# Narrow units of a two-block transformer kernel: eight high matmuls, then eight low ones

## What is computed

```python
p = einsum("bsd,de->bse", rms_norm(h), w_in)            # 2048 x 5120, then gates and two causal convolutions
h = h + rms_norm(einsum("bse,ed->bsd", mixed, w_out))   # 2048 x 2048
z = square(relu(einsum("bsd,df->bsf", m, w_up)))        # 2048 x 8192
h = h + rms_norm(einsum("bsf,fd->bsd", z, w_down))      # 8192 x 2048
# second block: w_in_a 2048 x 4096, pooling, 4 group matrices 512 x 512, w_out_a, w_k, w_v,
# w_in_b 2048 x 8192 (queries of 3 dilated attentions and a gate), attention, w_out_b
```

## Time and profile before

| | |
|---|---|
| median of 3 runs | 2077.09 us |
| profiled execution | 2077.38 us |
| its span, first to last instruction | 2075.6 us |
| TensorE matmul busy | 2035.1 us (98%), 11624 matmuls |
| weight loads busy, beside the matmuls | 1784.1 us (86%) |
| VectorE, ScalarE busy | 1410.5 us (68%), 1013.9 us (49%) |
| mean granted TensorE clock | 0.996 |

### The profile page before, as it was taken

How to read it: one execution, slowest core, us unless ns; L and a number is a source line. 1 busy time by engine, 2 the same in 40 slices (tenths; PEclk the granted TensorE clock), 3 DMA queues, 4 the chain that set the end, 5 groups by cost and what they waited for, 6 DMA issues and landing times.

```text
span 2075.6 us, 28620 instructions
## 1 busy us (share of the span) xinstructions
PE 2035.1 (98%) x11624; PEld 1784.1 (86%) x11624; DVE 1410.5 (68%) x1729; ACT 1013.9 (49%) x1348; POOL 9.8 (0%) x19
## 2 busy tenths in 40 slices
PE   6999999999999999999999999999999999999998
PEld 6999988988888888888879888788888888888886
DVE  5999956764655556555576766557577888887754
ACT  4676565544444444444454555445444455454542
POOL 0000000000000000000000000000000000000000
PEclk9999999999999999999999999999999999999999
DMA  6655646766666665666645565656566444544573
GB/s 219 195 185 164 193 136 226 234 200 192 194 190 195 189 194 188 190 194 189 195 132 183 162 194 186 226 172 223 188 191 192 153 160 145 183 146 160 179 261 107
DMA packets 305859, 384.27 MB, mean 185 GB/s; under 512 B 11673, under 2 KB 237209, under 8 KB 303936
## 3 DMA queue, kind: packets, MB, share of 16 engines
q1 hardware_dynamic: 305536, 382.22, 57.5%
q10 hardware_dynamic: 192, 0.23, 0.0%
HBM read 378.20 MB, written 4.19 MB: 184 GB/s over the span
## 4 chain that ended last, share of the span: by engine, by line
PE 93%; DVE 2%; issue 2%; ACT 1%; DMA 1%; SPq 0%; POOL 0%; DVEq 0%; POOLq 0%; ACTq 0%
PE job_banks L522 31%; PE job_banks L525 16%; PE job_banks L565 10%; PE job_banks L567 10%; PE job_banks L566 10%; PE job_banks L494 3%; PE job_banks L493 3%; PE job_banks L495 3%; PE aux_banks L747 1%; DMA raw_weights<-in_w_in 1%; ACT weights_high L812 1%; PE aux_banks L602 1%; DVE weights_low L1204 1%; PE aux_banks L567 0%; PE aux_banks L566 0%
## 5 line engine op out<-in xcount | busy, mean ns | idle before, releaser
L1204 DVE TENSOR_TENSOR weights_low<-raw_weights,weights_high 128x1024 fp32r<-128x1024 f32 x696 | 841.7, 1222 | 506.9 <-ACT weights_high L812 501.6
L812 ACT ACTIVATE weights_high<-raw_weights 128x1024 fp32r<-128x1024 f32 x696 | 728.3, 1056 | 621.7 <-PE job_banks L525 258.1
L522 PE MATMUL job_banks<-act_a,weights_high 128*128 128x512 f32 (+1 forms) x2048 | 610.1, 381 | 15.1 <-DVE weights_low L1204 6.6
L525 PEld LDWEIGHTS job_banks<-act_a,weights_low 128*128 128x128 f32 x2000 | 368.7, 191 | 74.1
L525 PE MATMUL job_banks<-act_a,weights_low 128*128 128x256 f32 (+1 forms) x2000 | 388.5, 276 | 0.0
L522 PE MATMUL job_banks<-act_b,weights_high 128*128 128x512 f32 x1088 | 345.6, 399 | 0.4 <-DVE value L1221 0.4
L522 PEld LDWEIGHTS job_banks<-act_a,weights_high 128*128 128x128 f32 x2048 | 315.2, 192 | 18.2 <-DVE weights_low L1204 9.7
L565 PE MATMUL job_banks<-weights_high,act_b 128*128 128x512 f32 x736 | 287.2, 390 | 2.0 <-DVE value L1221 2.0
L567 PE MATMUL job_banks<-weights_high,act_b 128*128 128x512 f32 x736 | 286.4, 389 | 0.0
L566 PE MATMUL job_banks<-weights_low,act_b 128*128 128x512 f32 x736 | 286.4, 389 | 0.0
L525 PEld LDWEIGHTS job_banks<-act_b,weights_low 128*128 128x128 f32 x1088 | 204.3, 188 | 48.3
(11 more groups left out here) (133 smaller groups left out, 1613.7 us busy)
## 6 DMA issues: line engine op xcount, KB each, us to landing
raw_weights<-in_w_up SPq DMA_DIRECT2D x128, 512.0 KB, 3.8
raw_weights<-in_w_down SPq DMA_DIRECT2D x128, 512.0 KB, 4.4
raw_weights<-in_w_in_b SPq DMA_DIRECT2D x128, 512.0 KB, 4.1
raw_weights<-in_w_in SPq DMA_DIRECT2D x80, 512.0 KB, 3.7
raw_weights<-in_w_in_a SPq DMA_DIRECT2D x64, 512.0 KB, 4.3
raw_weights<-in_w_out SPq DMA_DIRECT2D x32, 512.0 KB, 5.0
raw_weights<-in_w_out_a SPq DMA_DIRECT2D x32, 512.0 KB, 4.4
raw_weights<-in_w_v SPq DMA_DIRECT2D x32, 512.0 KB, 4.5
```

What stands on the lines that cost most here:

```text
L522: made = e.matmul(o_both, wh[:, k, f * P:(f + 1) * P], rhs, start=opens, stop=False)
L525: made = e.matmul(o[:, 0, low_toks], wl[:, k, f * P:(f + 1) * P], x[:, first + kt, 0, low_toks], start=False, stop=kt == job.tiles - 1)
L812: e.activation(high[:, s, :], raw[:, r, :], ACT.Copy).then_inc(*high_done.inc(n))
L1204: e.tensor_tensor(low[:, s, :], raw[:, r, :], high[:, s, :].bitcast(F32), ALU.subtract).then_inc(*low_done.inc(n))
```

## The change

In `narrow_unit` the loop over the banks `f` becomes the outer one, and the low matmuls get a loop of their own behind all high ones. A unit now has four high matmuls into bank 0, four into bank 1, then four low ones into bank 0 and four into bank 1. Its head waits for `high_done`, the low part for `low_done`; the bank of f = 1 is waited for before the fifth matmul, where it was before the second. The matmuls, their operands and their number stay. Unchanged are `direct_unit`, `wide_unit` and every other engine's code. Behind the change lines are moved: L522 is now L523, L525 is L529, and from `if halves[-1] == 1` on all are 4 further (L565 is L569, L602 is L606).

```diff
--- before.py
+++ after.py
@@ -504,24 +504,28 @@
                 x = bufs[buf]
                 toks = slice(halves[0] * P, (halves[-1] + 1) * P)
                 low_toks = slice(low_halves[0] * P, (low_halves[-1] + 1) * P) if low_halves else None
-                e.wait_ge(*low_done.at(n))
-                for k in range(job.per_unit):
-                    kt = u * job.per_unit + k
-                    for h in sorted(set(halves) | set(low_halves)):
-                        x_there(comes(first + kt, h))
-                    opens = kt == 0 and halves[0] == 0
-                    for f in range(2):
-                        bank = 2 * job.pair + f
+                e.wait_ge(*high_done.at(n))
+                for f in range(2):
+                    bank = 2 * job.pair + f
+                    o = banks[:, bank, :].rearrange("p (a n) -> p a n", a=2)
+                    for k in range(job.per_unit):
+                        kt = u * job.per_unit + k
+                        opens = kt == 0 and halves[0] == 0
+                        if f == 0:
+                            for h in sorted(set(halves) | set(low_halves)):
+                                x_there(comes(first + kt, h))
                         if opens:
                             bank_free(job, f)
-                        o = banks[:, bank, :].rearrange("p (a n) -> p a n", a=2)
                         if len(halves) == 2:
                             o_both, rhs = banks[:, bank, :], x[:, first + kt, :, :].rearrange("p a n -> p (a n)")
                         else:
                             o_both, rhs = o[:, :, toks], x[:, first + kt, :, toks]
                         made = e.matmul(o_both, wh[:, k, f * P:(f + 1) * P], rhs, start=opens, stop=False)
-                    for f in range(2 if low_halves else 0):
-                        o = banks[:, 2 * job.pair + f, :].rearrange("p (a n) -> p a n", a=2)
+                e.wait_ge(*low_done.at(n))
+                for f in range(2 if low_halves else 0):
+                    o = banks[:, 2 * job.pair + f, :].rearrange("p (a n) -> p a n", a=2)
+                    for k in range(job.per_unit):
+                        kt = u * job.per_unit + k
                         made = e.matmul(o[:, 0, low_toks], wl[:, k, f * P:(f + 1) * P], x[:, first + kt, 0, low_toks],
                                         start=False, stop=kt == job.tiles - 1)
                 if halves[-1] == 1:
```

## The result

The changed kernel takes **2079.68 us** (median of 17 runs, 2078.31 to 2082.53) against 2076.61 us of the kernel before (median of 17 runs beside it, 2075.47 to 2079.18). The ratio is 1.0015, 95% interval 1.0008 to 1.0022: **slower by 0.15%, 3.1 us**, where 3.9 us off were forecast. It lies 0.7 us above the upper end of the range. The profiled execution took 2080.73 us, its span is 2078.9 us.

The account below looks back on a forecast made before the run. The prediction took TensorE, in flight for 98% of the span, to bound the kernel. Its terms 3.3 + 0 + 0 + 0.6 = 3.9 us off gave 2073.2 us against the 2077.09 us median, with an 8-in-10 range of 2068.0 to 2079.0 us.

Parts of the forecast that it names:

- What bounds the kernel: Whole kernel: TensorE, in flight for 98% of the span, bounds the time; VectorE (68%) and ScalarE (49%) have slack.
- Part 1, the order: 344 full narrow units: four length-change cycles become one at 3.2 ns each, 3.3 us off; bounds 5.4 off to 1.4 on.
- the bound of 17 ns: Full narrow units: upper bound for a unit's one remaining cycle, -3 to +17 ns against 12.8 now; 1.4 us on.
- Part 2, by-half units: 36 unit passes of 256 and 128 columns: zero, 1.852 us a unit; bounds 12.9 us off, 2.4 on.
- Part 3, the weaker wait: Unit heads at the start and 369.75 us: earlier start lost before row scaling, zero; bounds 1.3 and 1.0 us off.
- The second place, at 369.75 us: Idle 1.00 us for low weights gets filled, but later transposes wait for row scaling: zero, bound 1.0 us off.
- Part 4, the second bank: Head of `pool_u` near 1075 us: three matmuls leave the stretch behind the wait, 3 x 0.213 = 0.6 us off.
- The rule beside it: Skill's matmul gap, columns / 2.4 + 2.5 ns whatever the neighbours: 650 ns a k tile in either order, order worth nothing.
- 512 columns keep their 235 ns: Rival, full units: 512-column matmuls stay at 233 ns while 256-column ones rise to 120; 13 us slower, 2090 us; chance 0.08.
- The order does not matter: Rival, full units: the 3.2 ns belong to operands, not length changes; only 0.6 us off, 2076.5 us; chance 0.20.
- the 0.10 for slower by over 0.2%: Whole kernel: chance of a slowdown over 0.2%, summed as 0.08 + 0.02.
- the 0.46 for no change: Whole kernel: chance of a time within 0.2% of before, summed as 0.28 + 0.20, less 0.02.

Follow-up runs that it names:

- e9: Changed kernel with the full units' low matmuls also at 512 columns, so no change of length in a unit: 2357.99 us, one execution.
- e4: Changed kernel with the two banks in turn within each eight matmuls instead of four and four: 2080.64 us, ratio 1.0015 to the kernel before.
- e8: Changed kernel with 26 matmuls nobody reads in the pause before the second half's transposes at the start: 2078.28 us, ratio 1.0005 to the kernel before.
- e10: Kernel before with 31, 15 and 17 filler calls in the pauses at 1075, 1204 and 1298 us: 2080.25 us, ratio 1.0013.
- e2: New order and wait in the by-half passes alone, full units as in the kernel before: 2077.45 us, ratio 1.0001.
- e3: Changed kernel with the old wait for low weights at the head of each unit: 2079.28 us, ratio 1.0011 to the kernel before.
- the six orders above: Full units with high and low in runs of one, two (before), three-three-two, four, eight (changed), sixteen: 2826, 2786, 2796, 2805, 2791, 2783 ns a unit.
- e13: Kernel before with 15, 7 and 8 filler calls in the pauses at 1075, 1204 and 1298 us: 2074.02 us, ratio 0.9988.
- e10 to e13: Four kernels with fillers in three later pauses, two also with sixteen-and-sixteen full units, new by-half passes and start filler: 2080.25, 2079.88, 2073.41, 2074.02 us.

## Why the prediction was wrong

- **What bounds the kernel**: right. The changed kernel is 98% TensorE, and every difference found is a duration or a pause of TensorE.
- **Part 1, the order: the step that failed.** It set "each cycle costs the same 3.2 ns" and took "3.3 us off". A cycle of eight and eight costs 17 to 19 ns, so a unit has about 19 where it had 13, and 2.1 us came on. The mechanism, a cost at the change of length and none in a uniform run, was right (e9, e4), its size as a function of the run was not. The evidence was there: the bound of 17 ns came from the 1.39 us of six wide matmuls behind 256-column ones, 0.03 us for one long run of 512 columns. A run of eight resembles that one more than a run of two, and the bound should have been the value. The sign of the part was wrong: 3.3 us off became 2.1 on, 0.7 beyond the part's own upper bound (1.4 us on). The unit of 2.793 us is none of those that the prediction named as signs, neither of being right (2.775 to 2.780) nor of being wrong (2.82, 2.786).
- **Part 2, by-half units, zero**: right. 1.85 us for eight and eight. A 128-column matmul among its like is no shorter, so neither bound was needed.
- **Part 3, the weaker wait, zero: the second step that failed, by 1.4 us in the mean of the traces and 2.4 in the profiled execution.** That the earlier start is lost in front of the row scaling was right, but the pause was said to grow to 1.6 us and to cost nothing. It grew to 3.08 us. Of these 2.7 us more, 1.1 are the earlier start and 0.5 a row scaling that came later in this execution (37.23 us against 36.73). The other 1.1 are there because TensorE was also through its slow beginning sooner: the first unit takes 3.47 us (19.03 to 22.50), the second already 1.97, the third 1.85, while in the kernel before the four matmuls of a k tile took 0.85 us until 26.13 us and 0.46 from 26.81 on. Behind the pause the clock fell, at a price of 2.0 us (e8) in that execution. (The size varies: e10, with the old order and wait in its by-half passes, has a pause of 1.78 us there and a stretch of 3.4 us at 0.50 behind it, so the kernel before isn't always free of it.) No time confirms this part by itself: those of e2 and e3 can't tell it from nothing. The second place, at 369.75 us, was worth nothing, as forecast. I counted when work waits, and not what a longer pause does to the clock behind it, though the earlier trace rows showed just that, a pause of 4 us and 0.50 behind it.
- **Part 4, the second bank**: the mechanism is right: four matmuls ahead of the wait, 0.35 us of idle time gone. The 0.213 us was a mean over two matmuls of 256 and two of 128 columns (1079.91 to 1080.77), not the price of the three of 256 that moved. e4 moves it back, but its time can't resolve 0.5 us.
- **The sum**: -3.9 forecast. By the parts as the traces have them: +2.1, 0, +1.4, -0.4 = +3.1, against +3.1 in time (1.7 to 4.6). With an interval that wide the agreement to the tenth is luck.
- **The rule beside it**: the Trainium skill's isolated gap (TensorE: Matmul & The Clock Gate, "Back-to-back issue gap"), columns / 2.4 + 2.5 ns, has no term for the neighbours. In a uniform run there is none either (e9), though at 226.7 ns and not 215.8 for 512 columns; between lengths the six orders above lie 9 to 52 ns a unit over the sum of their uniform rates.
- **The rivals.** "512 columns keep their 235 ns" had the sign but not the mechanism: they do go down to 226.7 in a run. "The order does not matter" is excluded by six orders with six different units. The loss is a fourth thing, what a long run of 512 columns pays behind 256-column ones. The 0.10 for slower by over 0.2% didn't come about, the measured 0.15% lies in the 0.46 for no change; but the range, which reached 1.9 us above no effect, had no room for two losses together.

## What to carry to other kernels

Do not scale the price of a change between kinds of work by the number of changes: read it where the trace has a run of the length in question, even if it is one place and the other is repeated a thousand times. Before an engine is allowed to start earlier, ask what it will wait for next: on TensorE a pause that grows from 0.4 to 3 us can cost half clock behind it, and work that nobody reads, sized to end inside the pause, gave 2.0 us back at one place (a trace, e8) and 2.7 us (0.6 to 4.4, e13) at three others.

## What I had not expected of the hardware

- The loss at a change between 512- and 256-column fp32r matmuls depends on the run: 6.6, 3.2, 9.7, 16, 19 and 19 ns a cycle for runs of 1, 2, 3, 4, 8 and 16. It falls on the 512-column matmuls behind the change. Neither the bank (e4) nor the second wait (e9) has a part. Why two and two is nearly free, and one and one isn't, stays open.
- Pauses of 1.8 to 2.8 us were followed by 3.4 or 6.8 us at a granted clock of 0.50 in some executions and by none in others (e2: 2.08 us, then 3.4; e10: 1.78, then 3.4; kernel before: 2.74 at 1916 us, none). All 13 pauses of 3.1 to 4.0 us in the traces, the first wait for data aside, were followed by one, and none of 1.7 us or less was. With the pauses filled, none was seen there (e8, e10 to e13).
- A matmul of 128 columns on fp32 operands runs as two of 0.11 us (62 for 31 in e10); on fp32r operands it is one (288 low matmuls of 128 columns in 36 unit passes of eight).
